# First cross attention: where the key weights are split, where the query operand is split, and where the token sum stands

## The reference, cut to what matters

```python
def rmsnorm(x, g):
    xf = x.astype(jnp.float32)
    y = xf * lax.rsqrt(jnp.mean(xf * xf, axis=-1, keepdims=True) + RMS_EPS)
    return (y * g.astype(jnp.float32)).astype(x.dtype)

def cross_attention(hn, mn, w_xq, w_xkv, w_xo):
    Bsz, S, _ = hn.shape
    M = mn.shape[1]
    q = (hn @ w_xq).reshape(Bsz, S, N_XHEADS, DH_X)
    kv = mn @ w_xkv
    k = kv[..., :D_MODEL].reshape(Bsz, M, N_XHEADS, DH_X)
    v = kv[..., D_MODEL:].reshape(Bsz, M, N_XHEADS, DH_X)
    s = jnp.einsum('bshd,bmhd->bhsm', q, k).astype(jnp.float32) * (DH_X ** -0.5)
    p = jax.nn.softmax(s, axis=-1).astype(v.dtype)
    o = jnp.einsum('bhsm,bmhd->bshd', p, v).reshape(Bsz, S, D_MODEL)
    return o @ w_xo

...
    for l in range(DEPTH):
        hn = rmsnorm(h, norm_mix_g[l])
        h = h + hybrid_mixer(hn, ...)
        hn = rmsnorm(h, norm_x_g[l])
        mn = rmsnorm(mem, norm_mem_g[l])
        h = h + cross_attention(hn, mn, w_xq[l], w_xkv[l], w_xo[l])
        hn = rmsnorm(h, norm_ffn_g[l])
        h = h + conv_glu(hn, w_up[l], conv_f_w[l], conv_f_b[l], w_down[l])
```

## Time and profile before

| what | us |
|---|---|
| median of three runs (lowest, highest) | 2977.14 (2973.89, 2978.42) |
| the profiled execution | 2975.67 |
| its span in the trace | 2973.9 |
| PE busy in that span | 2776.8 (93%) |
| last matmul of `out1` starts | 397.58 |
| first matmul of the keys starts | 402.93 |
| first matmul of the queries starts | 458.49 |
| last matmul of the queries starts | 556.09 |

### The profile page before, as it was taken

How to read it: one execution, slowest core, us unless ns; L and a number is a source line. 1 busy time by engine, 2 the same in 40 slices (tenths; PEclk the granted TensorE clock), 3 DMA queues, 4 the chain that set the end, 5 groups by cost and what they waited for, 6 DMA issues and landing times.

```text
span 2973.9 us, 36612 instructions
## 1 busy us (share of the span) xinstructions
PE 2776.8 (93%) x13206; PEld 2290.0 (77%) x13206; DVE 1824.1 (61%) x1930; ACT 1004.5 (34%) x1591; POOL 1359.7 (46%) x775
## 2 busy tenths in 40 slices
PE   8999888998999999999999988899997899999994
PEld 6888677887788888887887777677875788888883
DVE  7988451234876677766745547792379555555556
ACT  3257430232322222222324335353346222222222
POOL 4322303214566676665665330533143566566652
PEclk9999999999999999999999998999998999999997
DMA  3101232001121111112322110422023111111122
GB/s 143 36 29 43 85 102 68 29 34 65 32 64 46 50 52 57 53 46 102 115 92 79 43 36 1 163 87 70 19 94 103 43 56 57 52 46 53 60 71 95
DMA packets 70826, 191.20 MB, mean 64 GB/s; under 512 B 7632, under 2 KB 7888, under 8 KB 69712
## 3 DMA queue, kind: packets, MB, share of 16 engines
q1 hardware_dynamic: 59616, 152.92, 16.1%
q10 hardware_dynamic: 11120, 37.06, 3.3%
HBM read 172.65 MB, written 17.30 MB: 64 GB/s over the span
## 4 chain that ended last, share of the span: by engine, by line
PE 45%; issue 36%; POOL 13%; DVE 3%; DMA 1%; ACT 1%; POOLq 0%; SPq 0%; DVEq 0%; ACTq 0%
PE products L637 14%; PE products L1043 8%; PE others L1043 7%; PE products L1085 4%; PE others L1085 4%; POOL w_lo L549 4%; POOL w_lo L493 2%; POOL w_hi L490 2%; DMA w_raw<-wstream 1%; POOL w_raw L565 1%; POOL w_raw L567 1%; DVE work L2085 1%; POOL w_raw L556 1%; POOL part_sum L561 1%; PE products L739 1%
## 5 line engine op out<-in xcount | busy, mean ns | idle before, releaser
L549 POOL TENSOR_TENSOR w_lo<-w_raw,w_hi 128x512 fp32r<-128x512 f32 x328 | 449.3, 1375 | 462.6 <-ACT w_hi L1695 461.4
L1695 ACT ACTIVATE w_hi<-w_raw 128x512 fp32r<-128x512 f32 x328 | 207.3, 633 | 823.2 <-PE products L1043 216.7
L490 POOL TENSOR_TENSOR w_hi<-w_raw,small 128x1024 fp32r<-128x1024 f32 x58 | 117.6, 2027 | 680.7 <-PE products L637 385.7
L637 PE MATMUL products<-act_hi,w_hi 128*128 128x512 f32 x944 | 380.7, 403 | 17.7 <-DVE act_lo L2041 7.7
L637 PE MATMUL products<-act_lo,w_hi 128*128 128x512 f32 x944 | 371.5, 394 | 0.0
L637 PE MATMUL products<-act_hi,w_lo 128*128 128x512 f32 x944 | 371.4, 393 | 0.0
L493 POOL TENSOR_TENSOR w_lo<-w_raw,w_hi 128x1024 fp32r<-128x1024 f32 x98 | 258.2, 2635 | 162.7 <-ACT w_hi L1940 158.2
L637 PEld LDWEIGHTS products<-act_hi,w_hi 128*128 128x128 f32 x944 | 179.7, 190 | 63.0 <-issue 15.8
L637 PEld LDWEIGHTS products<-act_hi,w_lo 128*128 128x128 f32 x944 | 179.3, 190 | 38.6
L637 PEld LDWEIGHTS products<-act_lo,w_hi 128*128 128x128 f32 x944 | 179.7, 190 | 35.0 <-issue 0.2
L713 PE MATMUL products<-act_hi,w_hi 128*128 128x512 f32 x416 | 172.7, 415 | 21.6 <-DVE act_lo L2933 8.1
(11 more groups left out here) (510 smaller groups left out, 6826.3 us busy)
## 6 DMA issues: line engine op xcount, KB each, us to landing
w_raw<-wstream SPq DMA_DIRECT2D x155, 512.0 KB, 3.5
w_raw<-wstream SPq DMA_DIRECT2D x248, 256.0 KB, 2.6
work<-xT ACTq DMA_DIRECT2D x16, 512.0 KB, 8.2
parked<-work ACTq DMA_DIRECT2D x8, 512.0 KB, 2.6
work<-parked ACTq DMA_DIRECT2D x8, 512.0 KB, 10.2
parked<-work ACTq DMA_DIRECT2D x2, 2048.0 KB, 8.0
work<-parked SPq DMA_DIRECT2D x8, 512.0 KB, 7.9
out<-work ACTq DMA_DIRECT2D x8, 512.0 KB, 2.7
```

Source lines behind the costliest of these rows:

```text
L490: pool.tensor_tensor(w_hi[:, slot, :], w_raw[:, slot, :], zeros, ALU.add)\
L549: pool.tensor_tensor(ring_lo[slot], source, ring_hi[slot].bitcast(F32), ALU.subtract).then_inc(s(signal), 1)
L637: last = pe.matmul(out[:, c], a[:, ws, w], x[:, k, c], start=(k == 0 and i == 0), stop=(k == KT - 1 and i == 2))
L1695: act.activation(ring_hi[slot], source, ACT.Copy).then_inc(s("parts_high"), 1)
```

## The change

The first two key blocks are split before the last squares of `out1` (high part of block 0 ahead of the square of tile 6, of block 1 ahead of that of tile 7; their low parts after the additions of tiles 6 and 7). The relay covers 18 blocks: the first two query blocks are split by ACT and DVE too. Operand tiles 0 to 2 are split beside blocks 2 to 4, tiles 3 to 7 beside blocks 8 to 12. The value copies stand behind the low part of block 17. PE forms the token sum between keys and values. The rest is bookkeeping: the counts of `kv_high`, by which the second attention's blocks are numbered, grow by two, `KV0` and `high_outside` go, and `split_high` always waits.

```diff
--- before.py
+++ after.py
@@ -118,7 +118,6 @@
     for _of, _list in ((HALF_SQUARED, _second), (HALF_SUMMED, _summed)):
         for _item in [(_post, 0, _k) for _k in range(KT)] + _list + [(_next, 1, _k) for _k in range(KT)]:
             _of[_item] = len(_of) + 1
-KV0 = {"1": 0, "2": 2 * KT}
 XA0 = {"1": 0, "2": NCH}
 Y1_PARTS = [(0, None), (1, None), (4, 0), (5, 0), (6, 0), (7, 0), (4, 1), (5, 1), (6, 1), (7, 1), (2, None), (3, None)]
 FF0 = {"ffn1": 0, "ffn2": FT}
@@ -316,7 +315,6 @@
         half_of = lambda half: slice(half * HALF, (half + 1) * HALF)
         half_slot = lambda name, u: Gf[:, HALF * n_bank(name, u):HALF * (n_bank(name, u) + 1)]
         n_bank = lambda name, u: (u + 2) % 4 if name == "xo2" else 3 - u % 4
-        high_outside = lambda b: 16 + b - (BLOCK0["out2"] + 8) - (8 if not isinstance(b, int) or b >= BLOCK0["xo2"] else 0)
         z2_at = lambda n: Z2_AT["tile", n]
         mem_at = lambda n: Z2_AT["memory", n]
 
@@ -534,8 +532,8 @@
             split(18, 9, 0, used=14)
             split_third(19, (s("y1_lo"), 8))
             split_blocks(BLOCK0["out1"] + 3, BLOCK0["k1"])
-            relay(BLOCK0["k1"], BLOCK0["q1"], 0)
-            split_blocks(BLOCK0["q1"], BLOCK0["ffn1"] + 4)
+            relay(BLOCK0["k1"], BLOCK0["q1"] + 2, 0)
+            split_blocks(BLOCK0["q1"] + 2, BLOCK0["ffn1"] + 4)
 
             def parts(name):
 
@@ -595,9 +593,9 @@
                     free = (s("product_quarters"), 4 * (b0 + mem_at(n - 2) + 1)) if n >= 2 else (s("fin_totals"), 2)
                     split_between(b0 + at, mw_hi[:, n % 2, :], mw_lo[:, n % 2, :], free)
             split_blocks(BLOCK0["out2"], BLOCK0["out2"] + 8)
-            split_blocks(BLOCK0["out2"] + 8, BLOCK0["xo2"], lambda b: b + (16 - BLOCK0["out2"] - 8))
+            split_blocks(BLOCK0["out2"] + 8, BLOCK0["xo2"], lambda b: b + (18 - BLOCK0["out2"] - 8))
             split_blocks(BLOCK0["xo2"], BLOCK0["xo2"] + 8)
-            split_blocks(BLOCK0["xo2"] + 8, BLOCK0["ffn2"] + 4, lambda b: b + (16 - BLOCK0["out2"] - 16))
+            split_blocks(BLOCK0["xo2"] + 8, BLOCK0["ffn2"] + 4, lambda b: b + (18 - BLOCK0["out2"] - 16))
             parts("ffn2")
             for k in range(1, KT, 2):
                 pool.wait_ge(s("post_y"), k + 1)
@@ -1304,8 +1302,9 @@
             def attention(x):
                 if x == "1":
                     gemm("k1", 8, "m1", m_hi, m_lo, MEM)
+                    norm_sums("q1")()
                     value_gemm("v1")
-                    gemm("q1", 8, "q1", after_two=norm_sums("q1"))
+                    gemm("q1", 8, "q1")
                 else:
                     b, p = BLOCK0["q2"], PROD0["q2"]
                     for u in range(16):
@@ -1361,11 +1360,11 @@
 
                 act.wait_ge(s("consts"), 16)
 
-            def squares(name, src, ready, before_last=None):
+            def squares(name, src, ready, beside=None):
 
                 for k in range(KT):
-                    if k == KT - 1 and before_last:
-                        before_last()
+                    if beside:
+                        beside(k)
                     act.wait_ge(*ready(k))
                     if k >= 2:
                         act.wait_ge(*norm("squares_summed", name, k - 1))
@@ -1384,13 +1383,10 @@
                 act.wait_ge(s("product_quarters"), 4 * (b - 1))
                 act.activation(w_hi[:, b % 2, :], w_raw[:, b % 2, :], ACT.Copy).then_inc(s("kv_high"), 1)
 
-            def split_high(name, src, gain, ready=None, beside=None):
+            def split_high(name, src, gain, ready):
 
                 for k in range(KT):
-                    if beside:
-                        beside(k)
-                    if ready:
-                        act.wait_ge(*ready(k))
+                    act.wait_ge(*ready(k))
                     act.activation(act_hi[:, k, :], src(k), ACT.Identity, scale=col(gain, k)).then_inc(s("operand_hi"), 1)
 
             def load(dst, src, name):
@@ -1748,10 +1744,18 @@
             for k in range(KT):
                 load(W[:, k, :], ap["xT"][:, k, :], f"x_in{k}")
             memory("1")
-            squares("q1", h_tile, ev("out1"), lambda: weights_high("1", 0))
-            split_high("q1", h_tile, "x1", lambda k: (s("evacuated"), PROD0["k1"]), lambda k: weights_high("1", k) if k else None)
-            for n in range(KT, 2 * KT):
+            def query_high(k):
+
+                act.activation(act_hi[:, k, :], W[:, k, :], ACT.Identity, scale=col("x1", k)).then_inc(s("operand_hi"), 1)
+
+            squares("q1", h_tile, ev("out1"), lambda k: weights_high("1", k - 6) if k > 5 else None)
+            act.wait_ge(s("evacuated"), PROD0["k1"])
+            for n in range(2, 2 * KT + 2):
                 weights_high("1", n)
+                if 2 <= n < 5:
+                    query_high(n - 2)
+                elif KT <= n < KT + 5:
+                    query_high(n - KT + 3)
             roots("q1")
             cross("1")
             act.wait_ge(s("xa_out"), NCH)
@@ -2352,7 +2356,7 @@
             def weights_low(x, n):
 
                 ws = (BLOCK0["k" + x] + n) % 2
-                dve.wait_ge(s("kv_high"), KV0[x] + n + 1)
+                dve.wait_ge(s("kv_high"), n + 1)
                 dve.tensor_tensor(w_lo[:, ws, :], w_raw[:, ws, :], w_hi[:, ws, :].bitcast(F32), ALU.subtract)\
                    .then_inc(s("kv_low"), 1)
 
@@ -2366,16 +2370,6 @@
                 dve.wait_ge(s("product_quarters"), 4 * (BLOCK0["v" + x] + 4 * (g + 1)))
                 dve.tensor_copy(values_of[x][:, :, g * HALF:(g + 1) * HALF], slot("v" + x, g).rearrange("p (m f) -> p m f", m=2))\
                    .then_inc(s("evacuated"), 1)
-
-            def last_keys_and_values(x):
-
-                key(x, KT - 2)
-                weights_low(x, KT)
-                key(x, KT - 1)
-                for n in range(KT + 1, 2 * KT):
-                    weights_low(x, n)
-                for g in range(2):
-                    value(x, g)
 
             def query_tiles(x):
 
@@ -2637,13 +2631,21 @@
                 if name != "ffn1":
                     have_rstd(name)
 
-            to_tiles("out1", "q1", h_tile, True, lambda j: (s(f"x_in{j}"), 32), lambda: memory("1"))
-            for k in range(KT):
-                weights_low("1", k)
-                split_low("q1", k, h_tile, "x1")
-                if k > 1:
-                    key("1", k - 2)
-            last_keys_and_values("1")
+            to_tiles("out1", "q1", h_tile, True, lambda j: (s(f"x_in{j}"), 32), lambda: memory("1"),
+                     lambda j: weights_low("1", j - 6) if j > 5 else None)
+            for n in range(2, 2 * KT + 2):
+                if n < KT:
+                    weights_low("1", n)
+                if 2 <= n < 5:
+                    split_low("q1", n - 2, h_tile, "x1")
+                if 2 <= n < KT + 2:
+                    key("1", n - 2)
+                if n >= KT:
+                    weights_low("1", n)
+                if KT <= n < KT + 5:
+                    split_low("q1", n - KT + 3, h_tile, "x1")
+            for g in range(2):
+                value("1", g)
             have_rstd("q1")
             query_tiles("1")
             cross("1")
```

## The result

| | before | after |
|---|---|---|
| median of the runs, us | 2977.14 (2973.89 to 2978.42, 5 runs) | 2961.14 (2958.64 to 2966.87, 5 runs) |
| ratio, 95% interval | | 0.9948 (0.9937 to 0.9959) |
| profiled execution | 2975.67 | 2962.46 |
| span | 2973.9 | 2960.6 |
| end of `out1` to end of the queries | 158.51 | 145.30 |

The last line is the measure used from here on. It runs from the last matmul of `out1` plus its 0.23 to the last matmul of the queries plus 0.23 (397.81 to 556.32 before, 398.22 to 543.52 after), so that what an execution loses ahead of it or behind it doesn't blur it. It fell by 13.21, and so did the profiled execution. The two are equal to the hundredth by chance, since `out1` ended 0.41 later after; within that 0.4, all of the gain is made in this stretch and nothing behind it gives any back.

The account below looks back on a forecast made before the run. PE, busy in 93% of the span, was taken as the bound. Queries starting 5.0 earlier plus 8.9 in the query part gave 13.9 off the profiled 2975.67, 2961.8, taken as 2962; range 2958 to 2968.

Parts of the forecast that it names:

- The chain of ACT, DVE, relay and loads: Keys and values, block by block: spaced starts put the query start at 453.50, 5.0 earlier than 458.49.
- Both waits: PE's idle 4.96 between `out1` and the keys, and its 5.19 for `rstd` behind the token sum; both to go.
- that for the value copy behind low part 17: New PE wait before query tile 0, whose PSUM tile awaits that copy: about 4.3, against 2.39 before.
- the third part: Fewer operand tiles beside the keys: 1.0 of the 8.3 gained by the end of key 7.
- One slow stretch at the query start: A few us of PE at half clock behind its wait before the queries, priced at 2.0 in the query stage.
- the prediction's last sign: If the query start is right and the end isn't, the clock is wrong; if the start is late, the loads are.
- the load step: Low part n to high part n + 2 when the load comes last: 5.03, from block 12 on.
- The cover for `rstd`: Query stage: `rstd` exists by 456 and query tile 0 ends after 464, 8 us of cover.
- The 3.5 that the sum takes from the row: Time of one weight load, 3.5 of the 5.03 from low part n to high part n + 2.
- Late loads: Rival at the keys and values: loads of 4.4, not 3.5, query start 457.8, gain 9.6, 2966; chance 0.14.
- One more slow stretch: Rival, behind the wait at key 2 or at the query start: 1.7 to 2.2 each, 2964; chance 0.15.
- The slower case: Half clock all through the keys and values, making the kernel slower; chance 0.02.

Follow-up runs that it names:

- e3: Kernel after, with the copy of the first value product behind low part 13 instead of 17: 2958.83, ratio 0.9945.
- e6: Kernel after, loading only half the bytes of blocks 10 to 17, older numbers used for the rest: one execution of 2962.55, stretch 143.09.
- e1: Kernel before, with only the token sum moved between keys and values: 2968.31 against 2978.04, ratio 0.9967.
- e2: Kernel before, with only the early split of key blocks 0 and 1: 2974.93 against 2978.04, ratio 0.9993.
- e7: Kernel after, with 16 matmuls that nothing reads between values and queries, to keep PE busy: 2964.11, ratio 0.9953.
- e5: Kernel after, with copies of keys 0 to 2 ahead of the operand tiles beside blocks 2 to 4: one execution of 2965.88, stretch 142.90.
- e11: Kernel after, with first value copy behind low part 13, token sum behind key 1, copies of keys 0 to 2 ahead of operand tiles: 2956.02, ratio 0.9928.
- e4: Kernel after, unchanged, on the chip of three other runs for comparison: 2967.28, ratio 0.9965.
- e9: Kernel after, unchanged, repeated as the measure for three other runs: 2962.58, ratio 0.9955.
- e12: Kernel after, with only the token sum moved behind key 1, value copies left behind low part 17: one execution of 2964.26, stretch 143.28.
- e10: Kernel after, with first value copy behind low part 13 and token sum behind key 1, a repeat run: 2957.31, ratio to kernel before 0.9937.

## Why the prediction was right

All times of after here are less 0.41, by which its `out1` ended later.

| step | predicted | measured |
|---|---|---|
| first key behind `out1` | no wait | no wait |
| wait before key 2 | 1.8 | 1.85 |
| keys end | 424.02 | 424.51 |
| first value block | 425.90 | 425.83 |
| value block 9 | 428.63 | 428.99 |
| high part 17 | 449.98 | 449.86 |
| values end | 449.10 | 449.32 |
| queries start | 453.50 | 453.41 |
| query stage | 88.96 | 89.70 |
| gain in the stretch | 13.9 | 13.2 |

- **The mechanism was right step by step.** The chain of ACT, DVE, relay and loads, with a spacing for each step from one row of before, gave the query start to 0.1. Both waits went, and one that no row of before showed, that for the value copy behind low part 17, came where it was worked out. Experiment e3 confirms its cause, e6 that of the pace; e1 and e2 come near the gains expected of the parts. What the third part brings alone was argued, not run.
- **Mis-sized: the clock.** One slow stretch at the query start was forecast at 2.0; the query stage took 89.70, that is 2.5 over the 87.17 of e7. This is the 0.7 between 13.9 and 13.2, and it is the case that the prediction's last sign names: the query start right, the end not.
- **Mis-sized and made up for: the keys and the load step.** The keys ended 0.5 later than forecast: key 2 starts 0.2 late, as low part 2 does (403.18 less 0.41 against 402.57), and a key block, put at 2.88, takes 2.95 (413.12 to 424.92 for four). The token sum, put at 1.88, gives back a little of it: the first value matmul starts 1.32 behind it (424.92 to 426.24), but the second starts 0.64 behind the first, where 0.23 is normal, so the sum takes 1.32 + 0.41 = 1.73. Block 9 starts 0.36 late (429.40 less 0.41 against 428.63). The loads made up for that. From low part n to high part n + 2 they took 4.84, 4.96 and 4.82 on the way to block 17, and not 5.03. That these errors cancel, and leave the query start right to 0.1, is luck.
- **The cover for `rstd`** was 8 us by forecast. It was 11.3: ACT finished `rstd` at 456.12, and query tile 0 was done at 467.44 (its copy's start less 0.26).
- **The loads.** The 3.5 that the sum takes from the row held: they landed after 3.3, 3.5 and 4.4 (lowest, middle, highest) from 432 us on.
- **The rivals.** Late loads exist, one at a time: 1.0 to 1.3 in e7. One more slow stretch, behind the wait before key 2, came in e3 and e7 (1.4 each) and in none of the three executions of the kernel after. The slower case, to which the prediction gives 0.02, is half clock all through the keys and values; it was not seen in any run, and the granted clock of after is 1.00 from 412 to 440.
- **The median** fell by 16.0 and the forecast, 2962, was 0.9 above it. Two things of the same size meet in that. The forecast started from the profiled execution, 1.5 below the median; the prediction calls this half of the runs' spread, but the spread is 4.5 and 1.5 a third of it, and from the median the same sum gives 2963.2. And in the two later sets the kernel after is 10.8 and 15.3 below the kernel before, while the stretch is 13.0 below the one profiled execution of before each time: what moves the median by 2 or 3 either way lies in other stages (last section) and was not predicted. That the median is met within 1 is luck; that the stretch is met within 0.7 is not.

## What to carry to other kernels

Work out a reordering as a chain of starts, each step a spacing between two rows, and look for an instruction that is queued behind a wait it doesn't need: here a copy whose input was ready 15 us earlier held PE for 4 us and then cost 1.4 to 2.5 more in clock. The chain of loads, which sets the pace here, still starts where its first release comes from, so time won ahead of it was kept; "the loads will give it back" was wrong twice (1.65 won in the keys were 1.5 to 1.8 at the query start in e5, and 1.3 were 1.6 in e11). Put a short independent job (the token sum) into a wait that exists anyway; that, the earlier copy and the key copies first brought the stretch from 145.5 to 136.4, of which 2.5 is the slow stretch that is gone.

## What the runs showed of the hardware that was not expected

The same wait is not always followed by half clock (0.50 in slices of 1 us). At the query start 2.28 (e2) and 2.39 were, and 2.55 (e1) was not. The wait of 1.85 before key 2 was in e3 and e7, and was not in the kernel after, e4, e6 and e9, though all six run the same code up to there. Just behind the queries, outside the measure used here, every run has a wait of 2.63 for ACT. It was followed by half clock in e1, e5, e6, e7, e11 and e12 and not in the other eight. The kernel after and e5:

```profile
546.31 3.69 PE L976 MATMUL others<-work,tmp 128*128 128x256 f32 x16 [2.63 <-ACT tmp L1597]
```

```profile
544.21 5.38 PE L976 MATMUL others<-work,tmp 128*128 128x256 f32 x16 [2.63 <-ACT tmp L1597]
```

The same 16 matmuls take 1.7 more. So an execution that is spared a slow stretch at the query start can still have one just behind the measure, as e1 and e7 have. Between `out1` and the end of the queries, the waits of 3.65 to 5.19 were followed by half clock (0.50) each time. Its price behind such a wait at the query start was 2.4 to 2.5 in the kernel after, e4 and e9, and 1.4 to 1.6 in e5, e6 and e12.

The scatter between executions goes with the granted clock, as far as the traces show. The end of `out1`, long before the change, lies between 397.81 and 403.28. In one stretch of the mixer, 140 to 200 us, the granted clock is 0.97 where `out1` ends at 398.22 (the kernel after) and 0.91 where it ends at 403.28 (e10):

```profile
140.00:200.00 60.00, 56.55 (x330) 48.67 (x328) 53.62 (x94) 30.12 (x68) 14.92 (x6) 0.97 0.10 33
```

```profile
140.00:200.00 60.00, 56.99 (x317) 49.80 (x316) 50.28 (x79) 30.13 (x67) 14.23 (x7) 0.91 0.09 27
```

This stretch doesn't make all of the 5 us: the clock is 0.91 there in e1 and e12 too, where `out1` ends at 400.70 and 400.22. In e4 and e10, the two that end past 403, the clock from 60 to 140 us is lower as well, 0.94 against 0.96 in the kernel after. How much each stretch makes was not tested.
